# A two-block transformer kernel on one Trainium2 core: a new order of the opening's transfers and vector work, and a weight tile's lo part moved at the joints

## The reference

```python
for l in range(2):                                  # first block
    x = x + 0.5 * swiglu_ffn(rms_norm(x, ffn1_norm[l]), ffn1_w1[l], ffn1_w2[l])
    h = rms_norm(x, mix_norm[l])
    proj = h @ w_in[l]                              # three mixers: gated MLP, retention, sparse attention
    x = x + mix @ w_o[l]                            # mix: gated sum of the mixers' outputs
    x = x + 0.5 * swiglu_ffn(rms_norm(x, ffn2_norm[l]), ffn2_w1[l], ffn2_w2[l])
x = rms_norm(x, final_norm)
for layer in range(2):                              # second block: four mixers and a conv FFN
    x = x + merged @ w_out[layer]
    x = x + conv_ffn(rms_norm_2(x, norm_ffn_g[layer]), ...)
return rms_norm_2(x, final_norm_g)
```

## Time and profile before

| | |
|---|---|
| time of three runs, median (lowest to highest) | 2402.84 us (2400.41 to 2406.5) |
| the profiled execution: its time, its span | 2401.82 us, 2400.1 us |
| PE busy | 2363.1 us, 98% |
| DVE, ACT, POOL busy | 1391.8, 1138.0, 61.9 us |
| bytes moved by DMA | 407.13 MB, 170 GB/s over the span |
| granted TensorE clock, mean | 0.994 |

### The profile page before, as it was taken

How to read it: one execution, slowest core, us unless ns; L and a number is a source line. 1 busy time by engine, 2 the same in 40 slices (tenths; PEclk the granted TensorE clock), 3 DMA queues, 4 the chain that set the end, 5 groups by cost and what they waited for, 6 DMA issues and landing times.

```text
span 2400.1 us, 40143 instructions
## 1 busy us (share of the span) xinstructions
PE 2363.1 (98%) x17520; PEld 2233.6 (93%) x17520; DVE 1391.8 (58%) x1730; ACT 1138.0 (47%) x1595; POOL 61.9 (3%) x110
## 2 busy tenths in 40 slices
PE   8999999999999999999999999999999999999998
PEld 7999999999999999999999899999999999999998
DVE  4446656654454466565544655686655655685665
ACT  5435445454354354454543544355545444355543
POOL 0000000000000000000000100000000100000000
PEclk9999999999999999999999999999999999999999
DMA  6564543455555545334555434344555434345553
GB/s 249 181 216 176 198 141 124 158 176 185 184 176 183 214 176 198 129 124 170 209 187 182 158 137 145 135 147 176 185 188 181 159 141 150 131 158 182 178 190 109
DMA packets 60254, 407.13 MB, mean 170 GB/s; under 512 B 7696, under 2 KB 9232, under 8 KB 12464
## 3 DMA queue, kind: packets, MB, share of 16 engines
q1 hardware_dynamic: 60080, 404.58, 47.2%
HBM read 401.93 MB, written 2.10 MB: 168 GB/s over the span
## 4 chain that ended last, share of the span: by engine, by line
PE 89%; DVE 4%; ACT 2%; DMA 2%; issue 1%; POOL 1%; SPq 0%; POOLq 0%; ACTq 0%; DVEq 0%
PE bank L394 27%; PE bank L396 27%; PE bank L395 27%; DVE w_lo L206 2%; DMA w_raw<-in_tiles 2%; DVE hT_lo L342 1%; PE bank L1236 1%; PE bank L1631 1%; PE bank L1458 1%; PE bank L1318 1%; POOL x_rstd L276 1%; PE bank L1855 0%; ACT w_hi L198 0%; ACT a_sq L264 0%; PE bank L1881 0%
## 5 line engine op out<-in xcount | busy, mean ns | idle before, releaser
L394 PE MATMUL bank<-hT_hi,w_hi 128*128 128x256 f32 x3408 | 973.3, 286 | 2.2 <-ACT b_dv L805 1.3
L395 PE MATMUL bank<-hT_lo,w_hi 128*128 128x256 f32 x3408 | 965.6, 283 | 0.0
L396 PE MATMUL bank<-hT_hi,w_lo 128*128 128x256 f32 x3408 | 965.5, 283 | 0.0
L206 DVE TENSOR_TENSOR w_lo<-w_raw,w_hi 128x2048 fp32r<-128x2048 f32 x370 | 843.0, 2285 | 129.9 <-ACT w_hi L198 129.6
L198 ACT ACTIVATE w_hi<-w_raw 128x2048 fp32r<-128x2048 f32 x370 | 705.5, 1909 | 192.2 <-DMA w_raw<-in_tiles 192.0
L394 PEld LDWEIGHTS bank<-hT_hi,w_hi 128*128 128x128 f32 x3408 | 654.3, 192 | 7.5 <-issue 1.9
L395 PEld LDWEIGHTS bank<-hT_lo,w_hi 128*128 128x128 f32 x3408 | 654.5, 192 | 2.6
L396 PEld LDWEIGHTS bank<-hT_hi,w_lo 128*128 128x128 f32 x3408 | 654.3, 192 | 0.0
L615 DVE TENSOR_TENSOR a_ffn_g<-a_ffn_act,bank 128x256 f32<-128x256 f32 x88 | 37.1, 421 | 339.5 <-ACT a_ffn_act L567 339.4
L394 PE MATMUL bank<-w_hi,hT_hi 128*128 128x256 f32 (+1 forms) x736 | 214.9, 292 | 12.3 <-DVE hT_lo L342 9.9
L396 PE MATMUL bank<-w_hi,hT_lo 128*128 128x256 f32 (+1 forms) x736 | 211.6, 287 | 0.0
(11 more groups left out here) (336 smaller groups left out, 2794.6 us busy)
## 6 DMA issues: line engine op xcount, KB each, us to landing
w_raw<-in_tiles SPq DMA_DIRECT2D x370, 1024.0 KB, 4.8
a_cmp_w<-in_cmp_w SPq DMA_DIRECT2D x2, 2048.0 KB, 8.1
a_gm_rows<-in_rows SPq DMA_DIRECT2D x2, 768.0 KB, 6.8
x_res<-in_x SPq DMA_DIRECT2D x2, 512.0 KB, 4.9
rel_line<-a_line SPq DMA_DIRECT2D x1, 1024.0 KB, 8.9
a_ret_rows<-in_rows SPq DMA_DIRECT2D x2, 512.0 KB, 8.4
b_rows<-in_rows SPq DMA_DIRECT2D x2, 512.0 KB, 6.8
out<-x_res SPq DMA_DIRECT2D x4, 256.0 KB, 2.0
```

The source lines that it names most:

```text
L206: dve.tensor_tensor(k.lo[slot][:], k.raw[slot][:], k.hi[slot][:].bitcast(F32), ALU.subtract).then_inc(k.lo_done[slot], 1)
L394: pe.matmul(out, w[0], x[0], start=start, stop=False)
L395: pe.matmul(out, w[0], x[1], start=False, stop=False)
L396: return pe.matmul(out, w[1], x[0], start=False, stop=stop)
```

## The change

- In the opening SP issues the line's inputs before the identity and the columns, and tiles 0 and 1 are loaded ahead of x's half 1, in four pieces of 512 columns each, each with a semaphore of its own. ACT and DVE split these pieces one by one, in an order written out by hand, and PE waits for a piece at every second chunk.
- The line is made by one product on 4 partitions, one per head, and copied once. Its store reads each of the 4 partitions 128 times (a broadcast access pattern).
- DVE does xn of half 0 first of all. ACT's halving of a bias column table moves behind xn of half 1.
- In every joint the lo part of the next stage's tile 2 moves behind x's lo part of half 1.

```diff
 class Ring:
     def loads_to(self, sp, n):
         for m in range(self.loaded, min(n, len(self.places))):
             slot, at = self.slot[m], self.places[m]
+            if m < SPLIT:                               # SPLIT = 2
+                for q in range(PIECES):                 # PIECES = 4, PIECE = 512
+                    src = self.tiles[at:at + 1, :, q * PIECE:(q + 1) * PIECE]
+                    sp.dma_start(self.piece(self.k.raw, m, q), src.rearrange("a p n -> (a p) n")
+                                 ).then_inc(self.k.piece_in[m][q], 16)
+                self.loaded = m + 1
+                continue
...
+    def piece_hi(self, act, m, q):
+        act.wait_ge(self.k.piece_in[m][q], 16)
+        act.activation(self.piece(self.k.hi, m, q), self.piece(self.k.raw, m, q), ACT.Copy).then_inc(self.k.piece_hi, 1)
+    def piece_lo(self, dve, m, q):
+        dve.wait_ge(self.k.piece_hi, PIECES * m + q + 1)
+        dve.tensor_tensor(self.piece(self.k.lo, m, q), self.piece(self.k.raw, m, q),
+                          self.piece(self.k.hi, m, q).bitcast(F32), ALU.subtract).then_inc(self.k.piece_lo, 1)
+    def chunk_ready(self, pe, n, c):
+        if n >= SPLIT:
+            if c == 0:
+                self.ready(pe, n)
+        elif c % 2 == 0:
+            pe.wait_ge(self.k.piece_lo, PIECES * n + c // 2 + 1)
...
 class Join:
             if self.norm is not None:
                 self.norm.vector_xn(dve, t)
-                self.k.ring.lo_to(dve, self.end + 2 + t)
+                if t == 0:
+                    self.k.ring.lo_to(dve, self.end + 2)
                 self.norm.vector_lo(dve, t)
+        if self.norm is not None:
+            self.k.ring.lo_to(dve, self.end + 3)
...
 class Start:
-        self.line = r.at("line", 39040, [P, DIFF_HEADS, self.W])
+        self.line = r.at("line", 39040, [DIFF_HEADS, self.W])
...
         sp.dma_start(k.x[:, 0], x[:, 0]).then_inc(self.x_in[0], 16)
+        sp.dma_start(self.rel[:], w["rel"]).then_inc(self.rel_in, 16)
+        sp.dma_start(self.onehot[:], w["onehot"]).then_inc(self.rel_in, 16)
         sp.dma_start(k.ident[:], w["ident"]).then_inc(self.small_in, 16)
         sp.dma_start(self.cols1[:], w["cols1"].rearrange("l p n -> p l n")).then_inc(self.small_in, 16)
-        sp.dma_start(self.rel[:], w["rel"]).then_inc(self.rel_in, 16)
-        sp.dma_start(self.onehot[:], w["onehot"]).then_inc(self.rel_in, 16)
-        k.ring.loads_to(sp, 1)
+        k.ring.loads_to(sp, 2)
         sp.dma_start(k.x[:, 1], x[:, 1]).then_inc(self.x_in[1], 16)
         k.ring.loads_to(sp, 5)
-        sp.wait_ge(self.copied, DIFF_HEADS)
-        sp.dma_start(line_dram.rearrange("h p n -> p h n"), self.line[:]).then_inc(self.line_out, 16)
+        sp.wait_ge(self.copied, 1)
+        sp.dma_start(line_dram.rearrange("h p n -> h p n"),
+                     self.line[:].unsqueeze(1).broadcast_to([DIFF_HEADS, P, self.W])).then_inc(self.line_out, 16)
...
     def tensor(self, pe):
         pe.wait_ge(self.rel_in, 32)
-        for h in range(DIFF_HEADS):
-            pe.matmul(self.k.bank[4 + h][:], self.rel[:, h:h + 1].broadcast_to([32, P]), self.onehot[:], start=True,
-                      stop=True).then_inc(self.made, 1)
+        pe.matmul(self.k.bank[4][0:DIFF_HEADS, :], self.rel[:], self.onehot[:], start=True, stop=True
+                  ).then_inc(self.made, 1)
...
     def vector(self, dve):                              # new order
+        norm.vector_xn(dve, 0)
+        for q in range(2):
+            ring.piece_lo(dve, 0, q)
+        norm.vector_lo(dve, 0)
+        for q in range(2, PIECES):
+            ring.piece_lo(dve, 0, q)
+        ring.piece_lo(dve, 1, 0)
+        dve.wait_ge(self.made, 1)
+        dve.tensor_copy(self.line[:], k.bank[4][0:DIFF_HEADS, :]).then_inc(self.copied, 1)
+        for q in range(1, PIECES):
+            ring.piece_lo(dve, 1, q)
+        norm.vector_xn(dve, 1)
+        norm.vector_lo(dve, 1)
+        ring.lo_to(dve, 3)
     def scalar(self, act):                              # new order
+        self.root.scalar(act, 0)
+        ring.piece_hi(act, 0, 0)
+        norm.scalar_xn(act, 0)
+        ring.piece_hi(act, 0, 1)
+        act.wait_ge(self.small_in, 32)
+        norm.scalar_hi(act, 0)
+        for q in range(2, PIECES):
+            ring.piece_hi(act, 0, q)
+        for q in range(PIECES):
+            ring.piece_hi(act, 1, q)
+        self.root.scalar(act, 1)
+        norm.scalar_xn(act, 1)
+        act.activation(self.half_bias[:], ...)
+        norm.scalar_hi(act, 1)
+        ring.hi_to(act, 3)
```

More of the change, by code:

```diff
@@ L147, in __init__ @@
         self.used = [sem(f"w_used{i}") for i in range(SLOTS)]
+        self.piece_in = [[sem(f"w_piece{m}{q}_in") for q in range(PIECES)] for m in range(SPLIT)]
+        self.piece_hi, self.piece_lo = sem("w_piece_hi"), sem("w_piece_lo")
         self.res_ok, self.squared, self.rooted, self.xn_dve, self.xn_act, self.turned, self.hT_hi_ok, self.hT_lo_ok = (
@@ L158, in rsqrt @@
         pool.tensor_tensor(out, out, self.neg_half[:, 0:n], ALU.pow).then_inc(sem, 1)
+SPLIT = 2
+PIECES = 4
+PIECE = TILE // PIECES
 class Ring:
@@ L177, in close @@
         loads, count = [0] * SLOTS, [0] * SLOTS
-        for j, s in zip(self.slot, self.signals):
-            loads[j] += 1
+        for m, (j, s) in enumerate(zip(self.slot, self.signals)):
+            loads[j] += m >= SPLIT
             self.nth.append(loads[j])
@@ L191, in loads_to, with piece @@
             self.loaded = m + 1
+    def piece(self, parts, m, q):
+        return parts[self.slot[m]][:, q * PIECE:(q + 1) * PIECE]
+    def piece_hi(self, act, m, q):
+        act.wait_ge(self.k.piece_in[m][q], 16)
+        act.activation(self.piece(self.k.hi, m, q), self.piece(self.k.raw, m, q), ACT.Copy).then_inc(self.k.piece_hi, 1)
+        self.hi = m + 1
+    def piece_lo(self, dve, m, q):
+        dve.wait_ge(self.k.piece_hi, PIECES * m + q + 1)
+        dve.tensor_tensor(self.piece(self.k.lo, m, q), self.piece(self.k.raw, m, q),
+                          self.piece(self.k.hi, m, q).bitcast(F32), ALU.subtract).then_inc(self.k.piece_lo, 1)
+        self.lo = m + 1
+    def chunk_ready(self, pe, n, c):
[4 more added lines that the diff above has]
+            pe.wait_ge(self.k.piece_lo, PIECES * n + c // 2 + 1)
     def hi_to(self, act, n):
@@ L481, in first_up, with ready @@
         slot = k.ring.slot[n]
-        k.ring.ready(pe, n)
+        def ready(c):
+            k.ring.chunk_ready(pe, n, c)
+            if j == 0:
+                self.norm.ready(pe, t, c)
         last = tokens_major(pe, k, slot, t, self.ab[j][:, t * 256:(t + 1) * 256],
-                            (lambda c: self.norm.ready(pe, t, c)) if j == 0 else None)
+                            ready)
         if t:
@@ L2135, in vector @@
     def vector(self, dve):
[L2136 to L2144, removed]
-    def scalar(self, act):
[L2147 to L2158, removed]
+        k, norm, ring = self.k, self.norm, self.k.ring
+        norm.vector_xn(dve, 0)
[12 more added lines that the diff above has]
+        ring.lo_to(dve, 3)
+    def scalar(self, act):
+        k, norm, ring = self.k, self.norm, self.k.ring
+        self.root.scalar(act, 0)
[10 more added lines that the diff above has]
+        norm.scalar_xn(act, 1)
+        act.activation(self.half_bias[:], self.cols1[:, :, C1_BM:C1_BM + BRANCHES1 * KC], ACT.Copy, scale=0.5
+                       ).then_inc(self.halved, 1)
+        act.wait_ge(self.halved, 1)
+        norm.scalar_hi(act, 1)
+        ring.hi_to(act, 3)
     def pool(self, pool):
```

## The result

The changed kernel took 2414.94 us (median of 5 runs, 2414.26 to 2417.42) against 2403.21 us (2400.41 to 2407.31) for the kernel before on the same chip: the ratio is 1.0048, with a 95% interval of 1.0033 to 1.0063. It is 11.7 us slower. The forecast was 2415.6 us and slower, so the median came out 0.7 us from it. The profiled execution's span is 2412.5 us, 12.4 more than before.

A forecast was written before the change was run, and what follows sets the result against it. PE, busy 98%, was taken as the bound. +13.8 (tile 5), +2.6 (clock) and -3.6 (joints) made +12.8 on 2401.82 us: 2414.6, plus 1.0 for the median, 2415.6; own range 2408 to 2423, 8 in 10 2397 to 2423.

The forecast's parts named there:

- The opening: First product at 9.5 us instead of 17.27, half 1 at 20.3 instead of 30.86: 10.5 us earlier.
- rival (e): Opening gains less (late pieces or identity); nothing changes under the forecast, as the stall covers it; no chance given.
- D: Time of the line's transfer: 1.05 MB from 4 partitions at 27.3 GB/s, 38.4 us.
- the swap's halved rate: Swap transfers, 64 partitions each, ran at 205 GB/s where weight tiles have 401; read as groups of 8 partitions.
- (b): Few partitions cost the line's transfer nothing, or only confine it to four engines: no stall, 2388.7 us; chance 0.13.
- (c): Reads of few partitions limited, but repeats cheaper or other engines' work passes: 2397 to 2407 us; chance 0.11.
- (d): Line's transfer rate in proportion to partitions, 13.7 GB/s, taking 77 us: 2454 us; chance 0.04.
- Tile 5: Weight tile queued behind the line's transfer, reaching PE at 68.5 us instead of 54.68: +13.8, swallowing the opening's gain.
- The clock: After some 24 us idle for the late tile, PE restarts at half rate: +2.6 us (0 to 3.5).
- The joints: Nine joints, each distance from transposes to first product falling to 1.62 us: -3.6 us (0 to -6).
- The range: The forecast's own range for the whole kernel, 2408 to 2423 us, chance 0.72: D 36 to 45, clock, joints.

The follow-up runs named there:

- four_groups: Changed kernel with the line made on all 128 partitions, its store reading partitions 0, 36, 72 and 108, 128 times each: 2387.22 us against 2402.8 before, ratio 0.9928.
- one_group_16: Changed kernel with the line's store cut into four transfers of one row each, shared by 16 DMA engines: 2410.75 us against 2402.8 before, ratio 1.0032.
- joints_only: The kernel before with only the change in the joints: 2397.7 us against 2402.8, ratio 0.9973.
- all_groups: Changed kernel with the line made on 128 partitions and its store reading each of them four times: 2387.4 us against 2402.8 before, ratio 0.9929.
- two_groups: Changed kernel with the line made on 128 partitions, its store reading partitions 0, 32, 64 and 96: 2397.58 us against 2403.43 before, ratio 0.9979.

## Why the prediction was right, point by point

- **The opening.** Half 1 was put at 20.3 and came at 20.11; PE was ready for tile 5 at 44.1, where 44.2 was given. The first product, given as 9.5, came at 10.64: piece 0 was taken up by ACT at 7.74, not 6.5. It did not matter, since half 0 came to the high clock before its end (its last products lie 0.12 apart): it ended at 18.48, within the 17.5 to 19.7 given. So half 1 came 10.75 us earlier, 10.5 given, and rival (e) did not come.
- **The size of D.** The step from the swap's halved rate to "4 partitions are one group, 27.3 GB/s" held: 25 and 27 GB/s with 4 and with 16 engines. The section "Door 1: the DMA port swizzle" of the Trainium skill's page "SBUF — State Buffer", whose figure of 27.6 no run could be set beside then, agrees too. The 25 GB/s refute rivals (b), (c) and (d), which need 437 or 109, 35 to 53, and 13.7; four_groups and one_group_16 show that it is the partitions, and neither the repeats nor the number of engines. That a write to few partitions might be what halved the swap's rate stays possible beside this: no run here writes few.
- **Tile 5.** Given for 68.5, it came at 70.69, so the term is +16.0, not +13.8. Most of this is where the line's transfer stood: 6.47 MB, the bytes ahead of it, were moved at about 20.6 (312 GB/s up to there), not at 19.3 as in the kernel before, and it ended at about 59.5, not 57.7. In between lie some 39 us, so D was right. From there to ACT's start on tile 5 at 66.41 it is 6.9 us, 6.4 given. The prediction also let SP issue tile 5 at 23.5, with only the transfer waiting. In fact SP stood in its issues and came to tile 5 at 42.5. That was not foreseen, and by the sum it cost nothing here, as the line held its engines until 59.5.
- **The clock.** PE restarted at half rate and came to the high level at 76.6, 5.9 us later: 2.9 us lost, +2.6 given.
- **The joints.** -4.4 us by the distances (18.2 to 13.8), -3.6 given. The opening's 1.62, used as the floor, was itself 0.1 too long: 1.48 to 1.58 are reached.
- **The sum.** 16.0 + 2.9 - 4.4 = 14.5, and the spans differ by 12.4. The rest was not in the prediction. PE's slow-clock stretches in the two first mixing stages were shorter in the execution after. The stretch of before, then the one of after 15 us later, in which the same work lies:

```profile
295.00:320.00 25.00, 25.00 (x178) 25.00 (x176) 20.27 (x30) 11.91 (x14) 0.67 (x2) 0.80 0.46 170
950.00:985.00 35.00, 35.00 (x264) 35.00 (x263) 22.64 (x31) 13.90 (x16) 0.67 (x2) 0.85 0.39 142
```
```profile
310.00:335.00 25.00, 25.00 (x190) 25.00 (x188) 21.61 (x38) 12.57 (x14) 1.86 (x5) 0.86 0.54 200
965.00:1000.00 35.00, 35.00 (x278) 35.00 (x277) 22.64 (x31) 14.61 (x18) 0.67 (x2) 0.90 0.40 146
```

  25 x 0.06 + 35 x 0.05 = 3.3 us less lost, and one wait of 1.2 us at 1683 more: 14.5 - 3.3 + 1.2 = 12.4. Whether the change moved these clock stretches stays open. They do differ from one execution of the same kernel to the next: in 23 runs of the kernel before, next to the first experiments, the time goes with the mean granted clock, from 2397.56 us at 0.995 to 2411.06 at 0.989. So the terms given were together 1.7 us too small, and 2.1 us that were not in the prediction went the other way: that the median came within 0.7 us is luck, and the right mechanism is not.
- **The range.** Its low end, 2408, takes the favourable end of every term. Its high end, 2423, is D = 45 with the full clock cost and the joints at -3.6; with the joints at their bound of 0 it should have been some 2427.

Both parts of the change that were meant to help PE do: by the runs, the joints give 5 us (joints_only) and the opening some 10 more (all_groups); by the traces 4.4 and 11.1. One line of the change, the broadcast store, took back more than both.

## What to carry to other kernels

Before a transfer reads few partitions, ask how many groups of them it touches, and what stands behind it in its queue: here a store for which no compute engine waited held the next weight tile until 66, though its slot was free at 23. Keep the partitions that a bulk transfer touches spread over all 128, or give the slow transfer another queue. And when a transfer's source changes shape, price it anew even if its bytes are as before.

## What the runs showed of the hardware

- The issue of a transfer behind a slow one in the same queue takes long: the same table's issue took 0.62 us in all_groups, 7.58 in four_groups, 9.56 in two_groups and 15.22 in the changed kernel. The next three took some 2.1 us each in two_groups and 3.8 in the changed kernel. This shows as the length of the issue, not as a wait. That SP stands until the queues of the engines have room is the likely reason, and not shown.
- Four engines busy show as a share of 0.24 while the GB/s tell of the partitions: 25 GB/s at 0.24 (changed kernel), 53 at 0.26 (two_groups), 115 at 0.32 (four_groups), 27 at 0.90 (one_group_16). The two numbers together separate "few engines" from "few groups of partitions".
- With all 16 engines in slow packets PE stopped for 20.6 us without a named reason (one_group_16).
